# GpSimd takes part of VectorE's work around attention in a two-layer decoder trunk

## The reference

```
mod = silu(c) @ w_ada[l] + b_ada[l]            # 6 rows of 1024: shift, scale, gate, twice
h = x * (1 + sc1) + sh1
proj = h @ w_in[l]                             # qa ka va  qb kb vb  qi ki wi
qa, ka, qb, kb, qi, ki = rope(each, pos)       # (x1 cos - x2 sin, x2 cos + x1 sin)
ya = window_attention(qa, ka, va, sinks)       # 8 heads, 2 kv heads, window 128, causal
score = sum_h relu(qi . ki) * wi               # indexer, causal
yb = attention(qb, kb, vb) over the top 128 keys of each query by score
y = concat(rms_norm(ya) * g_a, rms_norm(yb) * g_b) @ w_o[l]
x = layer_norm(ALPHA * x + (1 + gt1) * y, ln1_g[l], ln1_b[l])
h = x * (1 + sc2) + sh2
y = (silu(h @ w_gate[l]) * (h @ w_up[l])) @ w_down[l]       # hidden width 2816
x = layer_norm(ALPHA * x + (1 + gt2) * y, ln2_g[l], ln2_b[l])
```

## Time and profile before

| | |
|---|---|
| Median of three runs | 1418.83 us |
| The profiled execution | span 1418.0 us |
| PE busy | 1302.7 us (92%) |
| DVE busy | 845.6 us (60%) |
| ACT busy | 511.3 us (36%) |
| POOL busy | 153.3 us (11%) |
| mean granted clock of TensorE | 0.964 of full |
| Chain that ended last | PE 68%, DVE 17%, ACT 5%, issue 5%, POOL 3%, DMA 2% |

### The profile page before, as it was taken

One profiled execution on the slowest core, in us unless ns is written; L12 is line 12 of the kernel. 1 busy time (PEld: TensorE's weight loads), 2 busy tenths in 40 slices (PEclk: granted clock), 3 DMA queues, 4 the chain that ended last, 5 costly groups with the idle time before them and its releaser, 6 DMA issues.

```text
span 1418.0 us, 18519 instructions
## 1 busy us (share of the span) xinstructions
PE 1302.7 (92%) x6392; PEld 1069.4 (75%) x6392; DVE 845.6 (60%) x1504; ACT 511.3 (36%) x1057; POOL 153.3 (11%) x199
## 2 busy tenths in 40 slices
PE   2799898899999999999999999889899999999996
PEld 2686776587888878888778677757698877888775
DVE  6668787738877756433166599873763345333327
ACT  0435355634333311223134555554453331132310
POOL 1080022100111100000003202200000000000001
PEclk9898799999999999999999989999999999999998
DMA  8553200412768735232123120011133233232211
GB/s 324 199 202 122 77 1 8 158 44 82 265 234 275 261 115 191 89 99 93 60 74 122 43 86 20 1 45 46 60 119 104 89 104 104 77 116 91 101 45 60
DMA packets 44273, 156.18 MB, mean 110 GB/s; under 512 B 5808, under 2 KB 5808, under 8 KB 44208
## 3 DMA queue, kind: packets, MB, share of 16 engines
q1 hardware_dynamic: 30528, 109.07, 22.9%
q0 software_dynamic: 12672, 46.14, 9.9%
q10 hardware_dynamic: 1008, 0.12, 0.1%
HBM read 153.21 MB, written 2.10 MB: 110 GB/s over the span
## 4 chain that ended last, share of the span: by engine, by line
PE 68%; DVE 17%; ACT 5%; issue 5%; POOL 3%; DMA 2%; SPq 0%; DVEq 0%; ACTq 0%; POOLq 0%
PE bank L480 20%; PE bank L482 20%; PE bank L481 20%; PE bank L692 2%; PE bank L656 2%; DVE pq L1360 2%; DVE top L1326 2%; DVE w_lo L1201 1%; DMA ada_w<-in_w_ada 1%; PE bank L635 1%; DVE scores L1332 1%; DVE ada_acc L1225 1%; DVE xs L1421 1%; DVE stats L1426 1%; DMA w_raw<-in_weights 1%
## 5 line engine op out<-in xcount | busy, mean ns | idle before, releaser
L480 PE MATMUL bank<-hT_hi,w_hi 128*128 128x512 f32 (+1 forms) x768 | 287.1, 374 | 2.2 <-issue 1.5
L482 PE MATMUL bank<-hT_hi,w_lo 128*128 128x512 f32 (+1 forms) x768 | 285.7, 372 | 0.0
L481 PE MATMUL bank<-hT_lo,w_hi 128*128 128x512 f32 (+1 forms) x768 | 285.7, 372 | 0.0
L1577 DVE TENSOR_TENSOR w_lo<-w_raw,w_hi 128x1024 fp32r<-128x1024 f32 x88 | 107.9, 1226 | 145.7 <-ACT w_hi L1107 145.7
L480 PE MATMUL bank<-w_hi,hT_hi 128*128 128x512 f32 (+2 forms) x448 | 173.5, 387 | 16.6 <-DVE hT_lo L1287 7.3
L481 PE MATMUL bank<-w_lo,hT_hi 128*128 128x512 f32 (+2 forms) x448 | 167.1, 373 | 0.0
L482 PE MATMUL bank<-w_hi,hT_lo 128*128 128x512 f32 (+2 forms) x448 | 167.0, 373 | 0.0
L480 PEld LDWEIGHTS bank<-hT_hi,w_hi 128*128 128x128 f32 x768 | 145.1, 189 | 28.1 <-issue 2.3
L481 PEld LDWEIGHTS bank<-hT_lo,w_hi 128*128 128x128 f32 x768 | 145.1, 189 | 25.1
L482 PEld LDWEIGHTS bank<-hT_hi,w_lo 128*128 128x128 f32 x768 | 144.9, 189 | 25.3
L939 ACT ACTIVATE w_hi<-w_raw 128x1024 fp32r<-128x1024 f32 x80 | 83.5, 1059 | 216.8 <-PE bank L482 213.8
(11 more groups left out here) (145 smaller groups left out, 1833.7 us busy)
## 6 DMA issues: line engine op xcount, KB each, us to landing
w_raw<-in_weights SPq DMA_DIRECT2D x184, 512.0 KB, 3.4
ada_w<-in_w_ada POOLq DMA_DIRECT2D x80, 512.0 KB, 5.0
ada_w<-in_w_ada SPq DMA_DIRECT2D x16, 512.0 KB, 5.1
xs<-in_x SPq DMA_DIRECT2D x4, 512.0 KB, 9.9
g_row<-in_ln_row POOLq DMA_DIRECT2D x4, 512.0 KB, 4.4
b_row<-in_ln_row POOLq DMA_DIRECT2D x4, 512.0 KB, 5.2
trunk_out<-xs SPq DMA_DIRECT2D x8, 256.0 KB, 2.1
modb<-in_b_ada ACTq DMA_DIRECT2D x1, 48.0 KB, 3.7
```

Of the source, the lines that this page charges most:

```text
L480: pe.matmul(dst, a_hi, b_hi, start=first, stop=False)
L481: pe.matmul(dst, a_hi, b_lo, start=False, stop=False)
L482: return pe.matmul(dst, a_lo, b_hi, start=False, stop=last)
L1577: nc.vector.tensor_tensor(w_lo[:, s, :], w_raw[:, s, :], w_hi[:, s, :].bitcast(F32), ALU.subtract).then_inc(lo_ready, 1)
```

## The change

Six things change. (1) GpSimd rotates chunk 2, in both layers, behind chunk 0 and the clearing of `kT`, instead of VectorE; in layer 1 the last four adaLN fetches of that part come behind it. (2) The key chunks 1 and 3 use `gt_row` as intermediate instead of `scratch` and count on a semaphore `keys_roped` of their own; `roped` counts chunks 0, 2 and 4. (3) `EARLY_ROUNDS` is 5, so 11 rounds are left in attention; rounds 2, 3 and 4 come ahead of chunk 3's rotation. (4) GpSimd multiplies each w_o piece by its gains, in place in `w_raw`, at the steps 32, 34, 36, 40, 46, 51, 56 and 61. ACT waits for that and rounds with one instruction. (5) The low parts of the first four w_o pieces are made by GpSimd, at the steps 42, 47, 52 and 57; those of the other four stay with VectorE, as one plain subtraction each. (6) In layer 2 GpSimd does the affine pass of the last layer norm, at the steps 0, 15, 23 and 31, in four operations of 512 columns per tile.

```diff
+GAIN_AT = (32, 34, 36, 40, 46, 51, 56, 61)
+AFFINE_AT = (0, 15, 23, 31)
-EARLY_ROUNDS = 3
+EARLY_ROUNDS = 5
...
+        def at_roped(l, c, t):
+            return (12 if c % 2 == 0 else 8) * l + 4 * (c // 2) + t + 1
...
+            parts = gt_row if c in (1, 3) else scratch
...
 (GpSimd)
+            def gain(l, j):
+                p = l * NP + WO_P + j
+                pool.wait_ge(raw_in[p % RING], 16 * (p // RING + 1))
+                for cols, g in gained(p):
+                    m = nc.gpsimd.tensor_scalar(w_raw[:, p % RING, cols], w_raw[:, p % RING, cols], g, None, ALU.mult)
+                m.then_inc(weight_gained, 1)
+            def gained_low_half(l, j):
+                p = l * NP + WO_P + j
+                pool.wait_ge(weight_gained, 8 * l + j + 1)
+                pool.wait_ge(hi_ready, p + 1)
+                nc.gpsimd.tensor_tensor(w_lo[:, p % RING, :], w_raw[:, p % RING, :],
+                                        w_hi[:, p % RING, :].bitcast(F32), ALU.subtract).then_inc(lo_ready, 1)
+            def affine(stage, t):
+                pool.wait_ge(row_in, 32 * stage)
+                pool.wait_ge(x_transposed, at_tile(stage, t))
+                for half in range(2):
+                    cols = slice(half * HALF, (half + 1) * HALF)
+                    m = nc.gpsimd.tensor_tensor(xs[:, t, cols], xs[:, t, cols], g_row[:, cols], ALU.mult)
+                m.then_inc(affine_scaled, 1)
+                pool.wait_ge(affine_scaled, t + 1)
+                for half in range(2):
+                    cols = slice(half * HALF, (half + 1) * HALF)
+                    m = nc.gpsimd.tensor_tensor(xs[:, t, cols], xs[:, t, cols], b_row[:, cols], ALU.add)
+                m.then_inc(affine_done, 1)
...
                 if l == 0:
+                    ada_fetch(4 * KD)
+                for t in range(T):
+                    rope(l, 2, t)
+                if l == 0:
                     ada_fetch(4 * KD + RING)
+                    pool.wait_ge(small_in, 16 * 6)
...
+                    if i in AFFINE_AT and l > 0:
+                        affine(2 * l, AFFINE_AT.index(i))
+                    if i in GAIN_AT:
+                        gain(l, GAIN_AT.index(i))
+                    if i in WO_AT:
+                        gained_low_half(l, WO_AT.index(i))
...
 (ACT, convert)
+                    if WO_P <= p % NP < WO_P + 8:
+                        act.wait_ge(weight_gained, 8 * l + p % NP - WO_P + 1)
+                    else:
+                        act.wait_ge(raw_in[p % RING], 16 * (p // RING + 1))
...
+                    nc.scalar.activation(w_hi[:, p % RING, :], w_raw[:, p % RING, :], ACT.Copy).then_inc(hi_ready, 1)
...
 (VectorE, attention)
-                    if i in WO_AT:
-                        convert(l, WO_P + WO_AT.index(i) + 1)
-                    if i in ASIDE_AT:
-                        k = ASIDE_AT.index(i)
-                        if l == 0:
-                            ada_group(4, k, k + 1)
-                        elif k % 2 == 0:
-                            affine(2 * l, k // 2)
+                    if i in ASIDE_AT and l == 0:
+                        ada_group(4, ASIDE_AT.index(i), ASIDE_AT.index(i) + 1)
+                conv[0] += 4
...
                 convert(l, C0P[4] + 1)
-                for t in range(T):
-                    rope(l, 2, t)
                 convert(l, C0P[4] + 2)
+                top_rounds(2, EARLY_ROUNDS)
                 for t in range(T):
                     rope(l, 3, t)
-                top_rounds(2, EARLY_ROUNDS)
```

More of the change, by code:

```diff
@@ L201, in build_trunk @@
         roped = sem("roped")
+        keys_roped = sem("keys_roped")
+        weight_gained = sem("weight_gained")
+        affine_scaled = sem("affine_scaled")
         rotated = sem("rotated")
@@ L325, in rope_views @@
             v = pk[:, t, 0:heads * HD] if c in (1, 3) else pq[:, (c // 2) % 2, t, :]
+            parts = gt_row if c in (1, 3) else scratch
             return heads, [a.rearrange("p (h d) -> p h d", h=heads)
-                           for a in (v, scratch[:, 0:heads * HD], scratch[:, 512:512 + heads * HD])]
+                           for a in (v, parts[:, 0:heads * HD], parts[:, 512:512 + heads * HD])]
         def rotate(engine, c, t):
@@ L435, in _ @@
                         ada_fetch(3 * KD + t + 1)
[L436 removed]
+                pool.wait_ge(roped, at_roped(l, 0, T - 1))
                 for g in range(KV_HEADS):
@@ L930, in convert @@
                     p = conv[0]
-                    act.wait_ge(raw_in[p % RING], 16 * (p // RING + 1))
+                    if WO_P <= p % NP < WO_P + 8:
+                        act.wait_ge(weight_gained, 8 * l + p % NP - WO_P + 1)
+                    else:
+                        act.wait_ge(raw_in[p % RING], 16 * (p // RING + 1))
                     act.wait_ge(piece_used, p + 1)
-                    if WO_P <= p % NP < WO_P + 8:
-                        for cols, gain in gained(p):
-                            m = nc.scalar.activation(w_hi[:, p % RING, cols], w_raw[:, p % RING, cols], ACT.Copy,
-                                                     scale=gain)
-                    else:
-                        m = nc.scalar.activation(w_hi[:, p % RING, :], w_raw[:, p % RING, :], ACT.Copy)
-                    m.then_inc(hi_ready, 1)
+                    nc.scalar.activation(w_hi[:, p % RING, :], w_raw[:, p % RING, :], ACT.Copy).then_inc(hi_ready, 1)
                     conv[0] += 1
@@ L1193, in convert @@
                     dve.wait_ge(hi_ready, p + 1)
-                    if WO_P <= p % NP < WO_P + 8:
-                        for cols, gain in gained(p):
-                            m = nc.vector.scalar_tensor_tensor(out=w_lo[:, p % RING, cols],
-                                                               in0=w_raw[:, p % RING, cols], scalar=gain,
-                                                               in1=w_hi[:, p % RING, cols].bitcast(F32),
-                                                               op0=ALU.mult, op1=ALU.subtract)
-                    else:
-                        m = nc.vector.tensor_tensor(w_lo[:, p % RING, :], w_raw[:, p % RING, :],
-                                                    w_hi[:, p % RING, :].bitcast(F32), ALU.subtract)
-                    m.then_inc(lo_ready, 1)
+                    if WO_P + 4 <= p % NP < WO_P + 8:
+                        dve.wait_ge(weight_gained, 8 * l + p % NP - WO_P + 1)
+                        dve.wait_ge(lo_ready, p)
+                    nc.vector.tensor_tensor(w_lo[:, p % RING, :], w_raw[:, p % RING, :],
+                                            w_hi[:, p % RING, :].bitcast(F32), ALU.subtract).then_inc(lo_ready, 1)
                     conv[0] += 1
@@ L1252, in gate_diagonal @@
                 if which == 0:
-                    dve.wait_ge(roped, at_chunk(l, 4, T - 1))
+                    dve.wait_ge(roped, at_roped(l, 4, T - 1))
                 else:
@@ L1292, in rope @@
                 dve.wait_ge(proj_evac, at_chunk(l, c, t))
-                if at_chunk(l, c, t) > 1:
-                    dve.wait_ge(roped, at_chunk(l, c, t) - 1)
+                if at_roped(l, c, t) > 1:
+                    dve.wait_ge(keys_roped, at_roped(l, c, t) - 1)
                 step(rotate(nc.vector, c, t))
-                rotate_sum(nc.vector, c, t).then_inc(roped, 1)
+                rotate_sum(nc.vector, c, t).then_inc(keys_roped, 1)
             def add_index_head(l, i, h):
@@ L1417, in residual @@
                 wait_phase(dve, l, q, t)
+                if q == WO0 and l > 0:
+                    dve.wait_ge(affine_done, at_tile(2 * l - 1, t))
                 nc.vector.tensor_tensor(ztmp[:], bank[BANKS[q] + t][:], gt_row[:, cols], ALU.mult)\
```

9 lines of the change are left out of this document (4 added, 5 removed).

## The result

The changed kernel takes 1422.05 us (median of 20 runs, 1416.11 to 1428.72) against 1417.28 (20 runs, 1414.13 to 1419.89): ratio 1.0026, 95% interval 1.0017 to 1.0036. It is slightly slower. 1399.4 had been forecast, with 1389 to 1411 as the range; the result lies outside it and on the wrong side.

What follows compares the result with a forecast made beforehand. It took TensorE and VectorE, both near full, to bound attention's first 40 steps, and VectorE's lateness the rest. -9.0 + 0.7 + 0.4 - 6.5 - 4.5 + 0.5 - 1.0 = -19.4 from 1418.83 gave 1399.4 us, range 1389 to 1411.

Steps and rivals of the forecast that it cites:

- Two more early rounds: Attention's first 40 steps: two selection rounds fewer there save 4.5 us a layer, -9.0 in both (-3.5 to -12).
- rival (a): In attention, TensorE and ACT are the bound already, so rounds bring 2 per layer; 1409 us, chance 0.2.
- The hand-over: Ahead of attention: GpSimd's chunk-2 rotation delays the first mask by 0.7 us in layer 2, 0.4 in layer 1.
- rival (c): Ahead of attention, GpSimd becomes the bound, its rotations slowed to 7.15 us each; 1423 us, chance 0.04.
- Rival (d): Attention starts 2 us later per layer, chunk 4's fourth rotation 3 late, cancelling the gains; 1415 us, chance 0.06.
- signs of being wrong: Attention: first section shortens under 2 us, second under 3, or TensorE waits over 3 a layer for GpSimd's rotations.
- w_o and affine: Attention after step 40: taking this work off VectorE removes TensorE's waits, -6.5 us in layer 2, -4.5 in layer 1.
- Roots can queue behind one gain or low part: GpSimd's loop in attention: roots delayed 2.6 us at most, against about a step of slack, cost 0.
- SP loads pieces 4 to 7: Attention: w_o loads, 3.4 us each, start after GpSimd's low parts, five steps ahead of their gains, cost 0.
- GpSimd's load: Attention: gains at 0.8 us per 512 columns, tight before chunk 4's fourth rotation in layer 2; +0.5 us (0 to +3).
- Key chunks' own scratch: Ahead of attention: chunk 1 can rotate beside chunk 0 but nothing is won; 0 us (0 to +2).
- Behind attention: After attention: w_o pieces 4 to 7 need one subtraction instead of two; -0.5 us per layer, -1.0 (0 to -2).

Runs made afterwards that it cites:

- e6: The kernel before with five early selection rounds instead of three, nothing else; 1425.66 us, ratio 1.0061.
- e10: e9 with five early rounds in layer 1 and three in layer 2; 1404.04 us, ratio 0.9909.
- e3: The kernel before with only chunk 2's rotation on GpSimd, the keys' own scratch and semaphore, and five early rounds; 1426.95 us, ratio 1.0063.
- e11: e10 with two early rounds in layer 2 instead of three; 1414.54 us, ratio 0.9979.
- e4: The changed kernel with layer 2's first affine tile at step 11 instead of 0; 1417.50 us, ratio 1.0000.
- e12: e9 with chunk 2's rotation on GpSimd and the third early round ahead of chunk 3's rotation; 1407.94 us, ratio 0.9943.
- e9: e2 with GpSimd's gains and affine tiles placed one at a time between chunk 4's rotations; 1404.01 us, ratio 0.9904.
- e2: The changed kernel with VectorE rotating chunk 2 again and three early rounds; 1413.53 us, ratio 0.9964.
- e5: e2 with the first affine tile at step 11 and the first four gains at steps 1, 2, 20, 29; 1410.38 us, ratio 0.9950.
- e8: e5 with layer 2's affine pass on VectorE again, at steps 42, 46, 50 and 54; 1411.60 us, ratio 0.9966.
- e7: The changed kernel with only the first four gains moved, to steps 1, 2, 20, 29; 1418.18 us, ratio 1.0006.
- e1: The changed kernel itself, unchanged, timed and profiled again; 1420.32 us, ratio 1.0019 against the kernel before.

## Why the prediction was wrong

**Two more early rounds (-9.0).** The step that failed, and the largest. It said "VectorE loses 5.9 of 61.5 us there. Then TensorE's 63.1 us is the larger load", and took 4.5 a layer from the idle time. VectorE did lose the time. But the two engines had stood near a balance, and VectorE was not the one that held the steps. e6 measures the term by itself: -3.7 in layer 1 and +1.4 in layer 2, or some -3.5 and +0.7 with the clock counted out; e10 gives -2.7 in layer 1. In e3, where GpSimd rotates, it is +0.5 and 0. These are single traces whose clocks differ, so the size in layer 1 is open between nothing and 3.7; none shows 4.5, and layer 2 shows none at all. That TensorE holds the steps fits this, but e11, where a round more costs 7.7, says that the other engine stood close behind. The rival (a), TensorE as the bound already, had the mechanism and priced it at 2 a layer; its 1409 needed a cheap hand-over. I had kept my lower end, 1.8, and then chosen above the named wait because short gaps are hidden under modelled ends. That reason is true of any stretch, so it was none for this one.

**The hand-over (+0.7 and +0.4, measured +6.6 and +3.6).** The step that failed is "The last query tile then lands between 842.5 and 844.9, VectorE's key rotations end at 844 to 845.5". The trace of after is 3.5 us early there: its first chunk-2 bank is emptied at 822.0 against 825.6. With that added the fourth rotation ended at 845.6, just outside, and the key rotations at 852.5, 7 us beyond the range. The meeting of GpSimd and VectorE was priced at "0.6 to 1.2 on VectorE", from two long subtractions in the earlier trace rows. The sixteen short key instructions were given nothing of their own, though rival (c) names them. It is their number that counts: six of them lasted about as long as the GpSimd instruction beside them. 5.6 us were added to the keys. The three subtractions took 6.08 instead of 3.5, 2.6 more. Against that stood the spare 2.7. The Trainium skill's rule (SBUF — State Buffer, Who interferes with whom), by which an instruction of one of the two engines takes their shared port whole, points to this answer, for the key instructions have two SBUF inputs; I applied it only to the rounds. The trace agrees for six of nine: 0.22 us alone, 1.30 beside GpSimd; three were not held.

A second thing was not weighed at all: the affine tile of "step 0" follows the rotations without a wait and lengthens the meeting, 3.8 us (e4). The parts do not add up one by one: in layer 2 two rounds alone cost 5.7 (e6), the rotation alone, with one round moved ahead of the keys, 2.3 (e12 against e9), both together 3.3 (e3). That the rotation makes the room that the rounds fill is the likely reason; it is argued and not shown.

Rival (c), GpSimd as the bound ahead of attention, is refuted in its own form: four rotations took 19.3 us, under its 24. Its result, 1423, is close for another reason. Rival (d), gain and loss cancel, named a later start of attention, a fourth rotation 3 us late and rounds worth little; that is what happened in kind (the rotation starts 69.1 us behind the first mask instead of 65.8), with a hand-over more than twice its 2 a layer. It had a chance of 0.06. Three of the prediction's signs of being wrong are met: first sections shortened by under 2 us, a second section by under 3 (layer 1), and TensorE waiting 7.8 us for GpSimd's rotations in layer 2.

**w_o and affine (-6.5 and -4.5, measured -9.0 and -2.5).** Right in mechanism in layer 2, and in sum, the latter in part by luck. No wait of VectorE for w_hi is left in 922:958, TensorE's for ACT's copies fell from 3.5 to nothing there. In layer 1 TensorE still waits 4.3 us for ACT's copies in 239:275 (3.4 before), and e2 and e5 show no gain there at all. The step that failed is "Roots can queue behind one gain or low part, 2.6 us at most, against about a step of slack" at a price of 0, and with it "SP loads pieces 4 to 7 ... five steps ahead of their gains: 0": GpSimd waits 9.0 us for these loads in layer 1, and ACT then 9.8 us for roots, 4.5 the longest, instead of 3.8. What this costs in time was not tried by itself. e8 splits layer 2: 6.2 from w_o, 2.8 from affine.

**GpSimd's load (+0.5, 0 to +3).** Mis-sized. A gain is 1.55 us per 512 columns, above my upper end of 1.28; moving the gains away is worth 2.1 us in layer 2 (e7 against e1). The place was named rightly, the fourth rotation behind an affine tile and three gains; with 1.55 the sum there is 15 us for the 11.1 that were free.

**Key chunks' own scratch (0).** Not tried by itself. e9 and the kernel before have hand-overs within 0.5 us of each other, so it costs next to nothing.

**Behind attention (-1.0).** -1.7 measured, 0.8 a layer, within its range.

**The median.** The two profiled executions show -3.3, the medians +4.8. In every execution of the changed kernel the time is 1.7 to 1.8 us above the span, so the span of 1418.0 belongs to one of the longest executions of the kernel before, and 1414.7 to the second shortest of the changed kernel's 20. The profile of e1 is a typical one (1419.92 us, clock 0.958). In it the six sections sum to -1.8 us against before, in after to -0.8. With the work behind attention the parts that the edit touches bring some 2.4 us in either, where 19.4 had been forecast. The medians are longer even so (+4.8 here, +2.3 for e1), so 5 to 7 us lie outside these parts.

There the clock of TensorE differs: over all timed runs its mean is 0.965 to 0.966 (median) in the kernel before and 0.958 in the changed kernel; within the changed kernel's 20 runs it goes from about 0.961 at 1416 us to 0.953 at 1429. A difference of 0.007 of 1420 us is 10 us of full-speed clock. By the estimate of e6, e1's trace loses 8.7 us more than that of before: 3.3 at layer 2's hand-over, 3.0 between layer 1's attention and layer 2's chunk 2, 1.8 behind layer 2's attention. Of these, after shows the first and the last, but not the second. All kernels with chunk 2's rotation on GpSimd and five early rounds have 0.958 to 0.960 (this one, e1, e3, e4, e7), all others 0.962 to 0.967, e9 the highest. That low clock stands beside a pause of TensorE is seen at the hand-over. The length of the pause is not the whole of it, for e6, with a hand-over as long, has 0.962. Why the clock is lower where both kernels do the same work stays open, and with it the cause of those 5 to 7 us.

## What to carry over

In this kernel GpSimd's rotations held up VectorE's instructions with two SBUF inputs (0.22 us became 1.30) and left its selection rounds alone (1.47 us for three MAX8 with and without them). Short instructions suffered most: count the instructions that overlap, not their time. Before crediting work taken off a loaded engine, find out which engine holds each step; here taking load from the other one brought little, and adding some cost a multiple. Small answers that another engine waits for, such as GpSimd's roots, must not queue behind work that waits for a load. In an in-order loop, place moved work behind a wait that ties it to a time: w_o's and the affine pass's edits belong to a kernel that is 0.3% slower in one placement, and to one that is 1.0% faster in another.

## What was not expected of the hardware

A VectorE multiplication of 128 x 64 took 1.30 us beside GpSimd and 0.22 alone; GpSimd's multiplication by a per-partition scalar, one input, took 1.55 us for 512 columns (1.62 on average), longer than its two-input multiplication (1.28). The Trainium skill (GPSIMD Engine Reference, When to use GPSIMD) calls one-input work there roughly line-rate; this row doesn't agree, since the one-input operation is the slower of the two. And one selection round too many in attention cost 7.7 us for 2.97.
